# Latent attention in a two-block transformer kernel: how the probabilities are turned and how the values are multiplied

## The reference, cut to what matters

```python
def one_block(args):                       # causal_block_attention, per block of 128 queries
    qblk, bi = args
    sc = jnp.einsum('bqhd,bkhd->bhqk', qblk.astype(jnp.float32), kf) * scale
    qpos = bi * Q_BLOCK + jnp.arange(Q_BLOCK)
    sc = jnp.where(kpos[None, :] <= qpos[:, None], sc, -jnp.inf)
    p = jax.nn.softmax(sc, axis=-1)
    return jnp.einsum('bhqk,bkhd->bqhd', p, vf)
...
return jnp.concatenate([h_ml, h_mla], axis=-1) @ w_out      # token_mixer
...
x = x + rmsnorm(mix, norm_post_mix[l])                      # second_block
m = rmsnorm(x, norm_pre_mlp[l])
y = jnp.square(jax.nn.relu(m @ w_up[l])) @ w_down[l]
x = x + rmsnorm(y, norm_post_mlp[l])
```

## Time and profile before

| what | us |
|---|---|
| median of 3 runs (lowest to highest) | 1540.59 (1539.43 to 1543.14) |
| the profiled execution's own time | 1543.34 |
| its span, first to last instruction | 1541.5 |
| PE busy over the span | 1509.8 (98%) |
| DVE busy over the span | 1126.3 (73%) |
| ACT busy over the span | 749.2 (49%) |
| POOL busy over the span | 654.2 (42%) |
| mean granted TensorE clock | 0.997 |

### The profile page before, as it was taken

The page is one execution under the profiler, slowest core; times in us unless marked ns, Lnnn a source line. Parts: engine busy times, 40 slices in busy tenths (PEclk is TensorE's granted clock), DMA queues, the critical chain, the costliest instruction groups (busy, mean ns, idle before and its releaser), DMA issues. The chain is left out here.

```text
span 1541.5 us, 20402 instructions
## 1 busy us (share of the span) xinstructions
PE 1509.8 (98%) x7106; PEld 1245.8 (81%) x7106; DVE 1126.3 (73%) x1849; ACT 749.2 (49%) x1259; POOL 654.2 (42%) x291
## 2 busy tenths in 40 slices
PE   9999999999999999999999999999899999999998
PEld 7888888778888877888888888767779878888887
DVE  5689999887875445777776768777744887677775
ACT  6554233454552445755544235554763745444444
POOL 3454444333344432344444645341533344555551
PEclk9999999999999999999999999999999999999999
DMA  5333333255443323333333133222103342333321
GB/s 208 96 123 96 97 98 100 93 159 147 156 150 97 97 80 109 101 104 109 110 96 96 49 96 96 82 69 69 35 21 96 139 121 89 101 98 110 97 95 55
DMA packets 46179, 155.74 MB, mean 101 GB/s; under 512 B 5124, under 2 KB 9348, under 8 KB 45832
## 3 DMA queue, kind: packets, MB, share of 16 engines
q1 hardware_dynamic: 45072, 150.95, 31.2%
q10 hardware_dynamic: 1016, 3.61, 0.7%
HBM read 147.20 MB, written 7.35 MB: 100 GB/s over the span
## 5 line engine op out<-in xcount | busy, mean ns | idle before, releaser
L578 POOL TENSOR_TENSOR w_lo<-w_raw,w_hi 128x1024 fp32r<-128x1024 f32 x191 | 473.2, 2487 | 517.2 <-ACT w_hi L1520 517.0
L704 PE MATMUL bank<-a_hi,w_hi 128*128 128x512 f32 (+1 forms) x1120 | 445.1, 397 | 2.7 <-DVE a_lo L3184 1.7
L704 PE MATMUL bank<-a_hi,w_lo 128*128 128x512 f32 (+1 forms) x1120 | 431.5, 385 | 0.0
L704 PE MATMUL bank<-a_lo,w_hi 128*128 128x512 f32 (+1 forms) x1120 | 431.1, 385 | 0.0
L1520 ACT CAST w_hi<-w_raw 128x1024 fp32r<-128x1024 f32 x199 | 204.7, 1046 | 181.5 <-DMA w_raw<-in_stream 181.2
L704 PEld LDWEIGHTS bank<-a_hi,w_hi 128*128 128x128 f32 x1120 | 210.5, 188 | 49.6 <-issue 3.9
L704 PEld LDWEIGHTS bank<-a_lo,w_hi 128*128 128x128 f32 x1120 | 210.6, 188 | 45.2 <-issue 3.4
L704 PEld LDWEIGHTS bank<-a_hi,w_lo 128*128 128x128 f32 x1120 | 210.4, 188 | 42.6
L588 POOL TENSOR_TENSOR dn_rest<-dn_raw,dn_first 128x1024 fp32r<-128x1024 f32 x13 | 31.4, 2417 | 276.0 <-DVE f_lo L2706 276.0
L704 PE MATMUL bank<-dn_rest,f_hi 128*128 128x512 f32 x364 | 141.6, 389 | 0.0
L1814 ACT CAST dn_first<-dn_raw 128x1024 fp32r<-128x1024 f32 x54 | 55.6, 1047 | 167.1 <-DVE dn_raw L2639 167.1
(11 more groups left out here) (434 smaller groups left out, 2858.1 us busy)
## 6 DMA issues: line engine op xcount, KB each, us to landing
w_raw<-in_stream SPq DMA_DIRECT2D x199, 512.0 KB, 3.6
dn_raw<-in_stream SPq DMA_DIRECT2D x56, 512.0 KB, 3.6
p_parts<-d_parts SPq DMA_DIRECT2D x8, 640.0 KB, 5.0
d_turned<-p_parts SPq DMA_DIRECT2D x32, 160.0 KB, 3.3
res<-in_xT ACTq DMA_DIRECT2D x1, 2048.0 KB, 9.0
out_y<-res_tok SPq DMA_DIRECT2D x8, 256.0 KB, 2.0
x_raw<-in_xT SPq DMA_DIRECT2D x3, 512.0 KB, 8.6
mem_raw<-in_memT SPq DMA_DIRECT2D x1, 1024.0 KB, 12.2
```

The source lines that it names most:

```text
L578: nc.gpsimd.tensor_tensor(w_lo[:, j, :], w_raw[:, j, :], w_hi[:, j, :].bitcast(F32), ALU.subtract).then_inc(w_lo_done, 1)
L704: return nc.tensor.matmul(o, l, r, start=start, stop=stop)
```

## The change

- The probabilities stay in PSUM after the exponentials (three banks, 4 to 6, in turn, where there were two), `latent_scaled(n)` on ACT writes them, multiplied by the reciprocal, to `l_probs` in SBUF.
- `latent_turn(n-1)` on DVE, placed behind `latent_inverse(n)`, turns them by 32x32 squares into `l_parts`.
- SP stores each unit's part in HBM (`latent_out`, each waits until the store before it has landed) and, after a head's fourth, reads the head back with four DMAs into `l_turned` (`latent_back`). Its loads of weight chunks in that stretch now stand between these at written places (`rings_at`).
- PE's transposes, `pair_turn` and the copies and scalings that belong to them go. `latent_values(h)` runs once per head, behind `ml_hook` of unit 4h+7 (head 7: of n = 34, among the first steps of WO): 10 matmuls with the values of the *pair* of heads as weights and 128 columns moving, features by tokens in bank 2, of which `latent_hi` (ACT) and `latent_lo` (DVE) take the 64 rows of this head, once per head instead of once per pair.
- The first step of the mLSTM values no longer waits until the bank of the first output gate has been copied.
- At the end, `end_out` of row block 2 is moved ahead of the adding of piece 6, and the gain products are separate (`end_gain`) and written later for the last three pieces.
- Addresses of some buffers change.

```diff
@@ sync @@
+            def rows_back(head, turned):
+                rows = p_parts[head].rearrange("(g i) (h n) -> h i g n", g=RING, h=RING)
+                for h in range(RING):
+                    sp.dma_start(turned[PART * h:PART * h + PART, :, :, :].rearrange("i g k j -> i g (k j)"), rows[h]
+                                 ).then_inc(sems["p_landed"], 16)
...
+            def latent_out(n):
+                h, qb = n // 4, n % 4
+                k = slice(part_of(qb, 0), part_of(qb, qb) + 1)
+                sp.wait_ge(sems["pT_ready"], 4 * MLA_G + n + 1)
+                sp.wait_ge(sems["p_stored"], 16 * (HEADS + n))
+                sp.dma_start(p_parts[HEADS + h].rearrange("p (g k j) -> p g k j", g=RING, k=TRIANGLE)[:, :, k, :],
+                             l_parts[:, :, k, :]).then_inc(sems["p_stored"], 16)
+
+            def latent_back(h):
+                sp.wait_ge(sems["p_stored"], 16 * (HEADS + 4 * h + 4))
+                if h == 0:
+                    sp.wait_ge(sems["gates_turned"], 1)
+                else:
+                    sp.wait_ge(sems["pv_done"], 4 * MLA_G + h)
+                rows_back(HEADS + h, l_turned)
+
+            rings_at = {6: (CH["OA"] + 5,), 7: (CH["OA"] + 6,), 8: (CH["OA"] + 7,), 9: (CH["WO"],), 14: (CH["WO"] + 1,),
+                        20: (CH["WO"] + 2,), 26: (CH["WO"] + 3,)}
+            for n in range(4 * MLA_HEADS):
+                latent_out(n)
+                if n % 4 == 3:
+                    latent_back(n // 4)
+                for c in rings_at.get(n, ()):
+                    ring(c)
@@ tensor @@
-                if k == 0:
+                if k == 0 and tb > 0:
                     pe.wait_ge(evac_dve, o - DVE_FROM)
...
             def latent_scores(n):
-                pe.wait_ge(sems["p_ready"], U0 + n - 1)
-                mla_score(MLA_G + n // 4, n % 4, ps[4 + n % 2][:, 0:(n % 4 + 1) * P]).then_inc(sems["s_ready"], 1)
-            def latent_turn(n): ...
-            def latent_values(n): ...
-            def pair_turn(p): ...
+                if n >= 3:
+                    pe.wait_ge(sems["p_scaled"], U0 + n - 2)
+                mla_score(MLA_G + n // 4, n % 4, ps[4 + n % 3][:, 0:(n % 4 + 1) * P]).then_inc(sems["s_ready"], 1)
+
+            def latent_values(h):
+                pe.wait_ge(sems["p_landed"], 16 * RING * (HEADS + h + 1))
+                pe.wait_ge(sems["o_ready"], MLA_G + h)
+                pair = slice(P * (h // 2), P * (h // 2) + P)
+                for qb in range(TB):
+                    for kb in range(qb + 1):
+                        m = mm(ps[2][:, qb * P:(qb + 1) * P].rearrange("p (g j) -> p g j", g=RING),
+                               v_mla[kb // 2][:, kb % 2, pair], l_turned[:, :, part_of(qb, kb), :], kb == 0, kb == qb)
                 m.then_inc(sems["pv_done"], 1)
...
             for n in range(4 * MLA_HEADS):
                 if n + 2 < 4 * MLA_HEADS:
                     latent_scores(n + 2)
-                turning = n >= 8 and n % 8 == 1
-                if n >= 8 and n % 8 == 2:
-                    latent_values(n - 2)
                 ml_hook(n)
-                if turning:
-                    pair_turn(n // 8 - 1)
-                latent_turn(n)
-                if n >= 1 and not turning:
-                    latent_values(n - 1)
+                if n % 4 == 3 and n >= 7:
+                    latent_values(n // 4 - 1)
                 ml_turns(n)
-            latent_values(4 * MLA_HEADS - 1)
-            pair_turn(MLA_HEADS // 2 - 1)
...
+                if n == 4 * MLA_HEADS + 2:
+                    latent_values(MLA_HEADS - 1)
@@ scalar @@
             def latent_exps(n):
                 act.wait_ge(sems["s_masked"], U0 + n + 1)
-                act.wait_ge(sems["pT_ready"], U0 + n - 1)
-                act.wait_ge(sems["p_inv"], U0 + n - 1)
+                if n >= 8:
+                    act.wait_ge(sems["p_inv"], U0 + n - 7)
+                o = ps[4 + n % 3][:, 0:(n % 4 + 1) * P]
+                A.activation(o, o, ACT.Exp, bias=negmax[:, n % 2:n % 2 + 1], scale=-1.0,
+                             accum_out=rowsum[:, n % 8:n % 8 + 1]).then_inc(sems["p_ready"], 1)
+
+            def latent_scaled(n):
+                act.wait_ge(sems["p_inv"], U0 + n + 1)
+                if n >= 1:
+                    act.wait_ge(sems["pT_ready"], U0 + n)
+                r = slice(0, (n % 4 + 1) * P)
+                A.activation(l_probs[:, r], ps[4 + n % 3][:, r], ACT.Copy, scale=rowinv[:, n % 8:n % 8 + 1]
+                             ).then_inc(sems["p_scaled"], 1)
+            def latent_hi(h): ...   # mix_hi rows of one head from ps[2], after pv_done
...
             for n in range(4 * MLA_HEADS):
-                if n >= 8 and n % 8 == 1:
-                    pair_hi(n // 8 - 1)
-                latent_turned(n)
+                if n % 4 == 0 and n >= 8:
+                    latent_hi(n // 4 - 2)
+                latent_scaled(n)
                 if n + 2 < 4 * MLA_HEADS:
                     latent_exps(n + 2)
                 ml_hook(n)
@@ vector @@
+            def latent_turn(n):
+                qb = n % 4
+                dve.wait_ge(sems["p_scaled"], U0 + n + 1)
+                if n >= 4:
+                    dve.wait_ge(sems["p_stored"], 16 * (HEADS + n - 3))
+                V.transpose(l_parts[:, :, part_of(qb, 0):part_of(qb, qb) + 1, :].rearrange("p g k j -> p k g j"),
+                            l_probs[:, 0:(qb + 1) * P].rearrange("p (k g i) -> p k g i", g=RING, i=PART)
+                            ).then_inc(sems["pT_ready"], 1)
...
             for n in range(4 * MLA_HEADS):
                 latent_inverse(n)
+                if n >= 1:
+                    latent_turn(n - 1)
                 if n + 2 < 4 * MLA_HEADS:
                     latent_mask(n + 2)
                 ml_first(n)
-                if n >= 1 and not turning:
-                    latent_scaled(n - 1)
+                if n % 4 == 0 and n >= 8:
+                    latent_lo(n // 4 - 2)
                 ml_rest(n)
...
-            for n in range(len(ENDS)):
+            for n in range(6):
                 end_add(n)
-                if n in (2, 4, 6):
+                end_gain(n)
+                if n in (2, 4):
                     end_out(n // 2 - 1)
+            end_out(TB - 2)
+            end_add(6)
+            end_add(7)
+            end_gain(6)
+            end_add(8)
+            end_gain(7)
+            end_gain(8)
             end_out(TB - 1)
```

More of the change, by code:

```diff
@@ L152, in z_at, with z_added, z_gained @@
     return KB + 2 * n
+def z_added(n):
+    return 2 * n + 1 if n < 6 else (13, 14, 16)[n - 6]
+def z_gained(n):
+    return 2 * n + 2 if n < 6 else (15, 17, 18)[n - 6]
 COLS = [("norm_mix_g", 8), ("b_gate", 16), ("conv_w", KB * TAPS), ("conv_b", 8), ("conv_ln_g", 8),
@@ L360, in program @@
         mix_lo = [a_lo[:, k, :] for k in range(KB)]
-        for k, hi, lo in ((4, B0 + 28672, B0 + 30720), (0, B0 + 2048, B0 + 4096), (5, C0 + 26624, C0 + 28672),
-                          (6, C0 + 30720, B0 + 10240), (1, G0 + 28800, B0 + 26624), (2, B0 + 6144, B0 + 8192),
+        for k, hi, lo in ((4, B0 + 28672, B0 + 30720), (0, B0 + 6144, B0 + 8192), (5, C0 + 26624, C0 + 28672),
+                          (6, C0 + 30720, B0 + 10240), (1, G0 + 28800, B0 + 26624), (2, C0 + 18432, C0 + 16384),
                           (3, BIAS0, BIAS0 + 2048), (7, BIAS0 + 4096, BIAS0 + 6144)):
@@ L365, in program @@
             mix_lo[k] = at(f"mix_lo{k}", [P, T], lo, F32R)[:, :]
-        o_rows = [at(f"o_rows{p}", [P, TB, P], o) for p, o in enumerate((C0 + 26624, C0, C0 + 4096, C0 + 8192))]
+        l_probs = at("l_probs", [P, T], TMP0 + 9216)
+        l_parts = at("l_parts", [P, RING, TRIANGLE, PART], TMP0 + 4096)
+        l_turned = at("l_turned", [P, RING, TRIANGLE, PART], B0)
         mixed = at("mixed", [P, KB, T], C0)
@@ L514, in parts_back @@
                     sp.wait_ge(sems["pv_done"], 4 * G)
-                rows = p_parts[G].rearrange("(g i) (h n) -> h i g n", g=RING, h=RING)
-                for h in range(RING):
-                    sp.dma_start(d_turned[PART * h:PART * h + PART, :, :, :].rearrange("i g k j -> i g (k j)"), rows[h]
-                                 ).then_inc(sems["p_landed"], 16)
+                rows_back(G, d_turned)
             first = CH["ATT"] + 8
@@ L548, in _ @@
                     ring(CH["FF1"] + 4 * (g + 1) + j)
-            for c in range(CH["FF1"] + UPS[0] + 4, CH["FF2"] + 4):
+            for c in range(CH["FF1"] + UPS[0] + 4, CH["OA"] + 5):
+                ring(c)
[20 more added lines that the diff above has]
+                for c in rings_at.get(n, ()):
+                    ring(c)
+            for c in range(CH["WO"] + 4, CH["FF2"] + 4):
                 ring(c)
@@ L2065, in _ @@
                 ml_hook(n)
-            pair_hi(MLA_HEADS // 2 - 1)
             for n in range(4 * MLA_HEADS, ML_END):
+                if n in (4 * MLA_HEADS, 4 * MLA_HEADS + 3):
```

(1 more changed line is left out.)

88 lines of the change are left out of this document (28 added, 60 removed).

## The result

| | before | changed |
|---|---|---|
| median of 5 runs, us (lowest to highest) | 1542.36 (1539.43 to 1543.38) | 1549.05 (1545.88 to 1550.99) |
| ratio changed / before (95% interval) | | 1.0045 (1.0033 to 1.0058) |
| profiled execution: its own time, span | 1543.34, 1541.5 | 1549.05, 1547.3 |
| mean granted TensorE clock | 0.997 | 0.991 |

The change makes the kernel 6.9 us slower (0.0045 x 1542, interval 5.1 to 8.9); the forecast was 8 us faster, 1532.5 with a range of 1520 to 1543.

What follows compares the result with a forecast made beforehand. The prediction took PE to bound the kernel and the latent stage. Its terms, -9.5 - 6.5 + 1.0 + 3.0 + 4.5 - 0.5, gave -8.0 us, hence 1532.5 us, with an 8-in-10 range of 1520 to 1543.

Steps and rivals of the forecast that it cites:

- PE's waits that go: Latent stage: PE's waits on `mix_lo`, `o_rows`, `probsT` and seven gaps' pipelined ends vanish: -6.5 us, bounds -5.2 and -10.
- PE's work: Latent stage: 96 transposes go, value records cost slightly more; net -9.5 us of PE time, bounds 0 and -9.5.
- DVE and ACT: Latent stage, 1040 to 1060: DVE gets even with PE, which stops the gain there: +1.0 us, bounds 0 and +3.
- Rival 4: Latent stage: POOL's subtractions hold up DVE's turns, PE waits for about 5 us of it: 1537.5 us; chance 0.05.
- The late weight chunk: Latent stage: OM 1's load, queued behind stores and readings, lands late for ACT and stops PE: +3.0 us, bounds 0 and +5.
- The round trip: Latent stage: turned probabilities go through HBM in 8.5 us; late for head 6, head 7 in time: +4.5 us, bounds 0 and +12.
- rival 3: SP's chained stores set the shortest unit: kernel about 1556 us at 4.0 us a unit, 1546 at 3.7; chance 0.10.
- The end: Kernel's end: moved `end_out` fills DVE's idle time, last add waits only for PE's last matmul: -0.5 us, bounds 0 and -1.

## Why the prediction was wrong, point by point

The sum was -9.5 - 6.5 + 1.0 + 3.0 + 4.5 - 0.5 = -8.0; measured +6.9.

- **The step that failed** is the half sentence under *PE's waits that go*: "the next scores give back, because they now wait for the first scaling on ACT: 0". It saw the new wait, priced it for the first unit alone and against a credit, and did not follow it through the 29 units that have it. `latent_scores` waits for `p_scaled`, which needs DVE's reciprocal at the head of its unit and, by the single buffer, the turn before. Price by runs: 6.8 us (1.0045 to 1.0001, interval 4.3 to 9.3), clock and a larger number of buffers included, and 11.4 us of waits in the trace. At unit 3 alone, where the credit was 0, a wait of 1.05 us went and one of 2.92 came.
- **PE's work, -9.5**: the records went as counted, but "Nothing hides this: PE is the bound" was wrong. PE at 111 of 120 us busy is near the bound, not on it: 5.3 us removed in the kernel before gave 3.7 (interval 1.7 to 5.7), and 8.8 us put back in the kernel with early banks cost 2.2. So in the kernel before most of it may have paid, while on the changed path the lower bound stated, 0, was nearer than the value taken.
- **PE's waits, -6.5**: they went (the earlier trace rows count six of them and not seven, which is 0.2 us), and `sT` (4.6 to 6.5 us in place of 2.4) and `ml_rows` (up to 5.2 in place of 0.5) grew in their place. The text had said that more than 3 us of new `sT` waits would mean that DVE is the bound; they grew by 2.2 us in the changed kernel and by 4.1 without the transfers, where lighter turns gained nothing, so it is not the load of the turns. That it is the order in which DVE, ACT and PE hand the mLSTM's parts on is the likely rest, and not shown.
- **DVE and ACT, +1.0**: DVE's load in the window grew by less than forecast (+6.4 for 9.4), ACT's by about as much (+6.6 for 6.8); in 1040 to 1060 DVE did get level with PE. The price of 5.6 us of turns is 0 within 3 us. Rival 4 did not come true for the turns, but the 2.27 us operation behind the longest wait ran and ended together with a subtraction of POOL.
- **The late weight chunk, +3.0**: the waits on chunks are there, but as five of 3.8 us together and not as one of 3 (the sixth of the six shown, 3.7 us at 1025, is in the kernel before as well). Taking them away by spread casts changed nothing, while the landings cost PE more in their place. They are not a term to be added to the round trip's.
- **The round trip, +4.5**: near in size, 4.3 us with the banks free early and 3.5 in the changed kernel, but both contain the late chunks, for which another 3.0 had been added, and the path was not the forecast one. In the changed kernel head 6 is late by 0.5 us and head 7, which was to be in time, by 1.8. With the banks free early heads 3, 5, 6 and 7 are late, by 0.9, 3.9, 0.5 and 1.8. The agreement in size is in part luck. The trip itself was shorter than reckoned: 2.45 us from a store's issue to the first read (1061.86 to 1064.31 in the changed kernel), 1.76 to issue the reads and 3.2 to land, 7.4 us in place of 8.5. The stores landed in 2.4 to 2.6 us, and rival 3 (a chain of stores) did not occur: DVE never waited for one.
- **The end, -0.5**: 0.5 in the trace, 1.5 (0 to 3.2) by runs.
- **Left out**: the clock at the start of the stage. The text looked at it after 1140 only, and credited nothing there, which held (0.83 before and after). But in 1030 to 1040 it was 0.85, and the first wait removed with the change is worth 4.6 us by runs and 2.9 by the traces in the kernel before; the change's new wait of 2.92 us takes it away again.
- **The size of the sum**: rival 3 adds 6.4 us at 3.7 us a unit, which is 1547 and not 1546. It changes nothing.

Put together by runs: the end and the first wait are worth -6.2 us (0.9960); the change with its banks free early stands at 0 and without the round trip at -4.2. So the new way of turning the probabilities costs 6 us net even with the bank mended (interval 3.7 to 8.9), and removing 96 transposes did not pay for it. Of these, 4.3 go with the transfers. The other 2 may be a longer chain through ACT and DVE; that is a difference of ratios from different kernels, uncertain by some 2.6 us, and not shown.

## What to carry to other kernels

When a step is moved behind another engine's work, write down for each buffer and bank which event freed it before and which frees it now, and in whose queue that event stands; here the two units from the scaling back to the exponential were worth 6.8 us, and without them 9.5 us of removed work did not show in the time. An engine that is 93% busy is not the bound of every unit: to price work removed from it, put idle work of the same size in or take some out and run it. And look at the granted clock behind TensorE's short waits before looking for work to remove.

## What the runs showed of the hardware

- Two waits of 1.05 us within 2 us took TensorE from 2.4 to 1.2 GHz (pitch of a 512-column matmul 0.23, then 0.43 us), one of 1.10 us did not; taking one of the two away was worth 2.9 us in the traces and 4.6 by runs. A single wait for a landing at head 7 went either way: behind 1.83 us in the changed kernel the 20 value records took 4.00 us, behind 1.82 us with the banks free early 2.50. The Trainium skill, TensorE: Matmul & The Clock Gate, section HAM oscillation — how this bites in real kernels, describes a kernel whose TensorE falls back to the lower clock at each wait for data and begins each next piece slow. The traces agree in kind: the 20 value records took 3.06 us four us behind a wait of 3.78, and 4.63 right behind one of 3.90, against 2.39. Where they differ is that here shorter waits did it too.
- The spread between runs of one kernel goes with the mean granted clock: of 128 runs of the kernel before, the 12 at 0.999 have a median of 1539.3 us, the 8 at 0.995 one of 1544.6.
- A VectorE operation on 128x4 elements took 2.27 us once, where the one just before, of the same size (L3039, 1123.36), took 0.28. It ran from 1123.67 to 1125.94, beside a subtraction of POOL from 1123.56 to 1125.92. That the one held the other was not tested.
